# Four buffers for raw expert weights, the root ahead of the low halves, indices copied early, and the routing of a pair of tiles over two steps

## What is computed

```python
for i in range(DEPTH):                      # DEPTH = 1
    mod = silu(c) @ ada_w[i] + ada_b[i]
    sh1, sc1, g1, sh2, sc2, g2 = split(mod, 6)
    hn = modulate(rmsnorm(x, norm1_g[i]), sh1, sc1)
    y = rglru_mixer(hn, ...)                # ends in (...) @ w_out
    x = x + g1 * y
    hn = modulate(rmsnorm(x, norm2_g[i]), sh2, sc2)
    x = x + g2 * grouped_moe(hn, router_w, router_b, w_gate[i], w_up[i], w_down[i])
return rmsnorm(x, final_norm_g)

def grouped_moe(h, ...):
    probs = softmax(h @ router_w + router_b)
    # best of 4 groups by the sum of its two largest, then the two best experts in it
    gates = ...                             # the two probabilities, normed to sum 1
    act = silu(h @ w_gate) * (h @ w_up) * gates     # for each expert
    return act @ w_down
```

## Time and profile before

| | us |
|---|---|
| three timed runs, median | 1388.31 |
| lowest and highest | 1386.82 and 1388.92 |
| profiled execution | 1389.41 |
| its span, first to last instruction | 1387.8 |
| PE busy in it | 1093.6 (79%) |
| DVE busy | 848.6 (61%) |
| POOL busy | 708.6 (51%) |
| ACT busy | 582.2 (42%) |
| mean granted clock of TensorE | 0.923 |

### The profile page before, as it was taken

The page is one execution under the profiler, slowest core; times in us unless marked ns, Lnnn a source line. Parts: engine busy times, 40 slices in busy tenths (PEclk is TensorE's granted clock), DMA queues, the critical chain, the costliest instruction groups (busy, mean ns, idle before and its releaser), DMA issues. The chain is left out here.

```text
span 1387.8 us, 21239 instructions
## 1 busy us (share of the span) xinstructions
PE 1093.6 (79%) x4860; PEld 878.0 (63%) x4861; DVE 848.6 (61%) x1217; ACT 582.2 (42%) x812; POOL 708.6 (51%) x752
## 2 busy tenths in 40 slices
PE   1359999999999992899999408487668778888881
PEld 0247778778778772788888406366556666666661
DVE  6994666766866845367776763355465655565653
ACT  1455667657667654122222103233343443343421
POOL 0555633633633600226676842156666666666653
PEclk9999999999999996999999658799898999999995
DMA  8446334335334125514545374366567667667642
GB/s 301 154 91 205 97 105 154 118 103 165 110 107 154 46 91 197 214 62 173 199 176 198 151 242 124 101 221 226 193 216 242 211 215 231 226 205 232 218 141 91
DMA packets 146301, 232.62 MB, mean 168 GB/s; under 512 B 34240, under 2 KB 101824, under 8 KB 145616
## 3 DMA queue, kind: packets, MB, share of 16 engines
q1 hardware_dynamic: 111248, 128.20, 28.5%
q0 software_dynamic: 23632, 62.49, 12.5%
q10 hardware_dynamic: 11376, 41.42, 9.2%
HBM read 177.45 MB, written 91.31 MB: 194 GB/s over the span
## 5 line engine op out<-in xcount | busy, mean ns | idle before, releaser
L1594 PE MATMUL e_gu<-w_hi,e_xh 128*128 x312 | 134.4, 431 | 37.0 <-DVE e_xl L1494 21.7
L1412 ACT ACTIVATE w_hi<-w_raw 128x1536 f32 x60 | 88.4, 1486 | 160.2 <-DMA w_raw<-in_moe_w_down_dram 96.8
L1275 POOL TENSOR_TENSOR w_lo<-w_raw,w_hi 128x1536 f32 x30 | 106.7, 3556 | 76.0 <-ACT w_hi L1412 39.0
L1596 PE MATMUL e_gu<-w_hi,e_xl 128*128 x312 | 127.7, 409 | 0.0
L1595 PE MATMUL e_gu<-w_lo,e_xh 128*128 x312 | 127.6, 409 | 0.0
L1157 PE MATMUL po<-wo_hi,b_yh 128*128 128x512 f32 x256 | 104.6, 408 | 27.8 <-DVE wo_lo L983 27.8
L1523 DVE SCALAR_TENSOR_TENSOR e_ob<-e_ab,e_rstd,e_fg 128x1024 f32<-128x1024 f32 x39 | 50.1, 1284 | 115.9 <-POOL e_rstd L1324 113.1
L543 DVE SCALAR_TENSOR_TENSOR XB<-xu,conv_w,XB 128x512 f32<-128x512 f32 x96 | 92.1, 960 | 42.3 <-ACT XB L413 38.7
L1617 PE MATMUL e_pd<-w_hi,e_ah 128*128 x156 | 71.3, 457 | 52.2 <-DVE e_al L1499 33.7
L636 PE MATMUL px<-hT_hi,wx_hi 128*128 128x512 f32 x256 | 101.7, 397 | 5.1 <-DVE wx_lo L477 5.1
L636 PE MATMUL pg<-hT_hi,wg_hi 128*128 128x512 f32 x256 | 104.3, 408 | 0.0
(11 more groups left out here) (272 smaller groups left out, 2862.4 us busy)
## 6 DMA issues: line engine op xcount, KB each, us to landing
e_xg<-hn_slots ACTq DMA_DIRECT2D x40, 512.0 KB, 4.9
e_xa<-x_slots ACTq DMA_DIRECT2D x39, 512.0 KB, 3.9
stg<-in_ada_w_dram POOLq DMA_DIRECT2D x32, 512.0 KB, 4.2
w_raw<-in_moe_w_gate_dram SPq DMA_DIRECT2D x32, 384.0 KB, 4.3
w_raw<-in_moe_w_up_dram SPq DMA_DIRECT2D x32, 384.0 KB, 5.0
n_ada<-in_ada_w_dram SPq DMA_DIRECT2D x16, 512.0 KB, 5.1
n_x<-in_x_dram SPq DMA_DIRECT2D x16, 512.0 KB, 3.3
hn_slots<-in_x_dram SPq DMA_DIRECT2D x16, 512.0 KB, 5.0
```

What stands on the lines that cost most here:

```text
L1275: tensor_tensor(w["lo"][:, ds(off + q * QW, QW)], w["raw"][:, q % 2], w["hi"][:, ds(off + q * QW, QW)].bitcast(F32), ALU.subtract).then_in ...
L1412: nc.scalar.activation(w["hi"][:, ds(off + q * QW, QW)], w["raw"][:, q % 2], ACT.Copy).then_inc(w["hi_done"], 1)
L1594: nc.tensor.matmul(gu[:], xh[:, tok], hi, start=(k == 0), stop=False)
L1596: last = nc.tensor.matmul(gu[:], xl[:, tok], hi, start=False, stop=(k == KD - 1))
```

## The change

- There are four raw weight buffers, one for each quarter. SyncE's loads of quarters 2 and 3 of expert 1 wait for nothing, and later quarters wait for the low half of the same quarter of the expert before. In the router stage the two added buffers lie over the projection's weights, so that quarters 2 and 3 of expert 0 are loaded behind the last `main`.
- In the expert stage GpSimd's root has four steps (the small constant of the norm is a column of its own behind e_ab, summed with the squares) and stands ahead of GpSimd's low half. The index columns are copied by `take_indices`, behind the low half, for the block to come.
- In the router stage DVE makes the logits of tile `s-1` in step `s`, behind `scale`; `softmax_in` and `choose` follow in even steps, `assign` and TensorE's `rank` come in odd steps. GpSimd sends one tile in each step, one step earlier than before. Behind the loop DVE makes the low halves of quarters 0 and 1 ahead of the last logits, and the last shift itself; quarters 2 and 3 are both DVE's, behind the tables. The residual rows of the last two tiles are sent last.

```diff
-            for s in range(1, NT + 1):
-                ...
+            for s in range(1, NT):
                 gate(s - 1)
-                if s >= 2:
-                    logits(s - 2)
-                if s >= 3 and s % 2 == 1:
-                    softmax_in((s - 3) // 2)
                 if s + 1 < NT:
                     low(s + 1)
                 if s >= 3 and s % 2 == 1:
-                    choose((s - 3) // 2)
-                if s >= 4 and s % 2 == 0:
-                    assign((s - 4) // 2)
-                if s < NT:
-                    scale(s - 1)
+                    assign((s - 3) // 2)
+                scale(s - 1)
+                logits(s - 1)
+                if s % 2 == 0:
+                    softmax_in(s // 2 - 1)
+                    choose(s // 2 - 1)
             g = NT // 2 - 1
+            gate(NT - 1)
+            low_w(0)
+            low_w(1)
             logits(NT - 1)
             softmax_in(g)
+            choose(g)
             scale(NT - 1)
-            choose(g)
+            dve.wait_ge(scaled, NT)
+            v.tensor_tensor(hn[:, (NT - 1) % RING], hn[:, (NT - 1) % RING], sh2[:], ALU.add).then_inc(last_shifted, 1)
             assign(g)
...
             for s in range(1, NT):
                 root(s - 1)
-                if s >= 5 and s % 2 == 1:
-                    send(s - 5)
-                if s >= 6 and s % 2 == 0:
-                    send(s - 5)
+                if s >= 4:
+                    send(s - 4)
                 shift(s - 1)
...
-                if s >= 4 and s % 2 == 0:
-                    rank((s - 4) // 2)
+                if s >= 3 and s % 2 == 1:
+                    rank((s - 3) // 2)
                 turn(s - 1)
...
             for q in range(2, NQ):
-                sp.wait_ge(w["lo_done"][q % 2], 3)
                 load_quarter(sp, io, w, 1, q)
             for b in range(E, MAXB):
                 load_rec(b)
             for e in range(2, E):
                 for q in range(NQ):
-                    sp.wait_ge(w["lo_done"][q % 2], 2 * e + q // 2)
+                    sp.wait_ge(w["lo_done"][q % 2], 2 * e - 1 + q // 2)
                     load_quarter(sp, io, w, e, q)
...
+                nc.gpsimd.tensor_tensor(root0[:], ssq[:], nhalf[:], ALU.pow).then_inc(rstd_step, 1)
...
+                nc.gpsimd.tensor_scalar(part[:], root0[:], ssq[:], root0[:], ALU.mult, ALU.mult).then_inc(rstd_step, 1)
...
+                nc.gpsimd.tensor_scalar(part[:], part[:], -0.5, 1.5, ALU.mult, ALU.add).then_inc(rstd_step, 1)
...
+                nc.gpsimd.tensor_tensor(rstd[:], root0[:], part[:], ALU.mult).then_inc(rstd_ready, 1)
...
-            with pool.Fori(3, nless) as i:
-                scatter_out(i - 2)
-                scatter_acc(i - 1)
-                low_w(pool, nc.gpsimd.tensor_tensor, i + 1, 1)
-                root(i - 1)
+            with pool.Fori(2, nless) as i:
+                scatter_out(i - 1)
+                scatter_acc(i)
+                root(i)
+                low_w(pool, nc.gpsimd.tensor_tensor, i + 2, 1)
+                take_indices(i + 1, i)
```

More of the change, by code:

```diff
@@ L861, in _ @@
                 squares(s - 1)
-                if s >= 3 and s % 2 == 1:
-                    exponent((s - 3) // 2)
                 evacuate(s - 1)
+                if s < NT and s % 2 == 0:
+                    exponent(s // 2 - 1)
             act.wait_ge(mm, NT)
             high_w(0)
+            high_w(1)
             exponent(NT // 2 - 1)
-            for q in range(1, NQ):
+            for q in range(2, NQ):
                 high_w(q)
@@ L1059, in _ @@
             done(v.tensor_scalar(tab["expert1"][:], eb[:], 1.0, None, ALU.add))
[L1060 to L1064, removed]
+            low_w(2)
+            low_w(3)
         @block.gpsimd
@@ L1113, in _, with send @@
             rows = lambda t: bass.IndirectOffsetOnAxis(ap=t, axis=0)
-            def send(it):
+            def send(it, rest=True):
                 r = it % RING
@@ L1125, in _ @@
                 root(s - 1)
-                if s == 5:
+                if s == 4:
                     pool.wait_ge(filled, 16)
-                if s >= 5 and s % 2 == 1:
-                    send(s - 5)
-                if s >= 6 and s % 2 == 0:
-                    send(s - 5)
+                if s >= 4:
+                    send(s - 4)
                 shift(s - 1)
-                if s == NT - 1:
-                    send(s - 4)
+            send(NT - 4)
             root(NT - 1)
-            send(NT - 4)
-            shift(NT - 1)
-            for it in range(NT - 3, NT):
-                send(it)
-            q = 2
-            pool.wait_ge(w["hi_done"], q + 1)
-            wcols = slice(q * QW, (q + 1) * QW)
-            nc.gpsimd.tensor_tensor(w["lo"][:, wcols], w["raw"][:, q % 2], w["hi"][:, wcols].bitcast(F32),
-                                    ALU.subtract).then_inc(w["lo_done"][q % 2], 1)
+            send(NT - 3)
+            for it in (NT - 2, NT - 1):
+                send(it, False)
+            for it in (NT - 2, NT - 1):
+                send_x2(it)
             for r in range(RING):
@@ L1200, in _ @@
                 main(s, 1, range(KD // 2, KD)).then_inc(mm, 1)
-            rank(NT // 2 - 2)
             turn(NT - 1)
@@ L1274, in low_w @@
                     eng.nop(nofuse=True)
-                    tensor_tensor(w["lo"][:, ds(off + q * QW, QW)], w["raw"][:, q % 2],
+                    tensor_tensor(w["lo"][:, ds(off + q * QW, QW)], w["raw"][q][:],
                                   w["hi"][:, ds(off + q * QW, QW)].bitcast(F32),
@@ L1419, in square @@
                 act.nop(nofuse=True)
-                nc.scalar.activation(squares[:], ab[:], ACT.Square, scale=1.0 / 32, accum_out=ssq[:]).then_inc(squared, 1)
+                if first:
+                    act.wait_ge(halved, 2)
+                nc.scalar.activation(squares[:], ab_eps[:], ACT.Square, scale=1.0 / 32, accum_out=ssq[:]).then_inc(squared, 1)
             load_h(0)
@@ L1683, in build @@
             w["y" + n[0]] = [over(f"b_y{n[0]}{u}", [P, D], (KD + u) * D) for u in range(2)]
+            if n == "lo":
+                w["raw"] += [over(f"w_raw{q}_0", [P, QW], WE + (q - 2) * QW, F32) for q in (2, 3)]
             for i, name in enumerate(("gy", "hT") if n == "hi" else ("g1row", "sh2")):
```

116 lines of the change are left out of this document (62 added, 54 removed).

## The result

The changed kernel takes 1420.38 us (median of four, 1417.57 to 1423.09), the kernel before 1388.62 beside it (1386.82 to 1390.25): a ratio of 1.0229, 95% interval 1.0202 to 1.0256. The forecast was 1401 with a range up to 1416. The direction was right, the time is 19 us beyond the forecast and outside the range. The profiled execution took 1418.5 us with a span of 1417.0, 29.2 more than the span before.

A forecast was written before the change was run, and what follows sets the result against it. TensorE was taken to bound the router stage, GpSimd's queue and its lock with DVE the expert stage. From 1389.4, terms 31.9 + 6 - 4.6 - 9.7 + 5 - 15 - 1 gave 1402.0, forecast 1401 us, range 1352 to 1416.

The forecast's parts named there:

- In the walk: Expert stage: engine chains followed through the new order, giving +5 for two-block experts, -15 for three-block ones, -1 at the drain.
- Router loop: Router stage: choose spills past the next gate and is stopped by GpSimd's shift, 31.9 us, plus 6 for the clock.
- The signs that it named: Profile afterwards: TensorE waits at turn and rank, choose instructions over 2 us, router stage some 38 us longer.
- I take 1 us for each of the six long waits: Router loop: the turn runs slower at the lower granted clock after long waits, 6 us, between 0 and 10.
- End of the router stage: DVE's chain behind the last matmul gets shorter: -4.6 us, between -8 and 0.
- Start of the expert stage: With four buffers SyncE's records and loads wait for nothing and end sooner behind the barrier: -9.7 us.
- ScalarE's waits for weights are worth nothing in a step: Expert stage: removing ScalarE's 96.8 us of weight waits alone gains nothing, since GpSimd's own queue starts its next low half.
- pairs (+5): Expert stage, about nine experts of two blocks: no gain expected, +5 us, from -5 to +12.
- 33.5 us for three steps instead of 36.4: Expert stage, some five experts with a third block, where GpSimd without a low half catches up: -15 us.
- the lock costs more than it did: Rival, expert stage: every e_ob is caught, paired steps take 14.5 us, three-block experts gain nothing; 1425 us, chance 0.09.
- The rival of 1349: Expert steps escape the DVE-GpSimd lock and cost GpSimd's own work alone, 4.9 us less a pair; chance 0.16.

The follow-up runs named there:

- early copies alone: The kernel before with only the index columns copied behind the root for the block to come, ahead of both scatters: 1360.62 us, ratio 0.9804.
- two buffers: The kernel before, two raw buffers kept, with GpSimd's root in four steps behind its low half and index copies a block ahead: 1349.29 us, ratio 0.9718.
- root behind: The changed kernel with its router loop put back and GpSimd's root put back behind its low half: 1335.46 us, ratio 0.9624.
- old loop: The changed kernel with its router loop put back as in the kernel before, all else kept: 1379.37 us, ratio 0.9934.
- e1: The changed kernel with only its router loop put back; router tail, four buffers and expert stage stay: 1379.37 us, ratio 0.9934.
- the second experiment: The changed kernel with GpSimd's shift moved ahead of its sends in the router loop: 1393.72 us, ratio 1.0053.
- the first experiment: The changed kernel with the router loop of the kernel before, its tail, buffers and expert stage unchanged: 1379.37 us, ratio 0.9934.

## Why the prediction was right in direction and too small in size

The runs split the change, along one path. Each line is the difference of two ratios, times 1387 us, and by their intervals uncertain by some 5 us. "In the walk" means that the prediction has no price of its own for the part: it walked through all of the expert stage's steps at once and came to -11 us.

| part of the change | from, to | us | forecast |
|---|---|---|---|
| index copies a block ahead | before, early copies alone | -27 | in the walk |
| root in four steps | early copies alone, two buffers | -12 | in the walk |
| four buffers, new end of the router stage | two buffers, root behind | -13 | -14.3 |
| root ahead of the low half | root behind, old loop | +43 | in the walk |
| router loop | old loop, changed kernel | +41 | +37.9 |
| sum | | +32 | +12.6 |

The three parts in the walk come to +4 us for -11. By the two traces the sum is 16.6 us above the forecast's (29.2 for 12.6): 1.4 us from before the router loop, 2.3 from the loop, 1.8 from the end of the router stage, 1.5 from the wait for records, and 9.6 from the rest of the expert stage.

**Router loop: right in mechanism and in sum, with two errors that cancel.** The signs that it named are there: waits at rank and turn in six steps, a small instruction of `choose` of 3 us, a loop 40 us longer. Its makeup was different. The stall is 3.9 us and not 4.9, since `choose` alone spills 1.3 to 1.7 us and not 2.5; six of them and a first of 1.3 make 25 us for 31.9. The clock took nearly all of the rest, some 14 us for the 6 reckoned: besides the turn the half main behind it ran slowly, 3.7 to 4.6 us instead of 3.0, so that each long wait cost some 2.4 us more. The term "I take 1 us for each of the six long waits" was mis-sized, and its upper end of 10 too. That the loop came out 2 us from its 37.9 is luck: 7 too many for the stall, 8 too few for the clock.

**End of the router stage: right in sign.** -2.8 us for -4.6 (the prediction's own items against it, 2 + 1.3 + 1.3 - 2.9, make 1.7 and not 2.0). Low halves and tables were done at 856.2, but the barrier let go at 863.9; before it GpSimd's ten scatters of the last pair were issued up to 853.1. That their landing ends the stage now is read from this order, no run tested it.

**Start of the expert stage: right.** DVE's wait fell from 19.85 to 11.03, TensorE's start moved 8.2 us for 9.7. 16 records in 17.52 us and 32 in 36.24 are 1.1 us each, and nothing else is left of it.

**ScalarE's waits for weights are worth nothing in a step: right.** 85.7 us of them are in a kernel that is 2.8% faster than before. The one place where two buffers still cost is the expert with a single block, 3.1 us.

**Expert stage: the step that failed.** The prediction walked through the new order as a whole and found nothing for pairs (+5) and, for an expert with a third block, "33.5 us for three steps instead of 36.4", -15 in all. Pairs came out right: 27.3 to 28.6 us between scatters of the output, 27.3 to 28.2 before. The three-block experts take 34.4 to 38.4 us, all seven together 258.9 where they took 257.6: nothing is gained. (There are seven of these and six pairs, where the prediction said five and nine.) With the part of the stage before and behind them, the term of -11 us measured -1.4. What the walk lacked is the far end of e_ob: its buffer is released by a scatter that is now issued behind the low half, and DVE waits 27.9 us for such landings in the whole run, where it waited for none before. It also took e_ab at 1.23 us, where it is 2.39 in the mean. The run with e_y in PSUM shows what that costs: with e_ab free, the seven take 244.8 us instead of the 259.4 of e1. What the late scatter costs apart from e_ob's own stop stays open. The rival *the lock costs more than it did* gave 1425, 5 us from the result, but partly by chance: it charged 19 us to pairs, which cost nothing more, left out half of the clock, and took 10 us for the lost gain of the three-block experts, where the forecast's own term was 15. What it had right is that the three-block experts gain nothing.

**What the walk hid.** The worse mistake is not in the result but in the reasoning: moving the root and moving the copies were costed as one, "it is inside these walks". Apart, they are +43 and -27 us. By the prediction's own rows a step of GpSimd lost 0.2 + 0.87 us by the copy ahead of the sum's scatter; times 26 steps with weights that is 28 us, and the early copies alone measured 27.

**The rival of 1349** (steps free of the lock) wanted GpSimd's low half less than 8 us behind e_ob. The order with the root behind meets that (5.8 us, 1104.59 to 1110.43), as the kernel before did (7.7 us). In the changed kernel it starts 11.2 us behind the e_ob of 1172.22, for 9.8 reckoned, so late that it runs into the next e_ob and e_ab (1183.41, 0.8 us behind that e_ob's start). With the early copies and four buffers the order of before gives 1335 us: the move of the root took away the condition on which this rival stood.

## What to carry to other kernels

An instruction that locks another engine out is placed by what the other engine does at that moment: GpSimd's low half is free beside DVE's work with an operand in PSUM and costs 3 us beside work on two SBUF operands. 43 us hung on the order of one queue, by the lock and by the late scatter together. Cost each moved step alone before you walk through all of them together; two edits of opposite sign hide each other. A wait of an engine that disappears (here DVE's for the root) is worth nothing if that engine does not set the step, and a scatter that is issued late holds its source buffer: e_ob waited 3.61 us for one.

## What was not expected of the hardware

- With one operand in PSUM DVE's addition of 128x1024 takes 1224 ns in the mean, where it took 1.23 us unstopped: leaving the lock costs nothing of its own.
- In the changed kernel's loop the granted clock fell after all six waits of TensorE of 2.5 us; in the second experiment it fell after two of seven waits of 1.3 to 1.7 us, with nothing in the rows that tells the two from the five. The fall lasts into the matmuls behind the turn, and costs about as much again as the wait at the turn. It doesn't always come at once: behind the loop of the first experiment the turn that followed a wait of 2.78 us ran in 1.09 us at a granted clock of 1.00, and only the matmuls from 779 us on were at 0.50.
- GpSimd's root of one element a partition took 2.22 us beside DVE's two low halves, for 0.57 to 0.62 where DVE has no such work, and DVE's instruction of 8 elements 2.95 us for 0.17. The Trainium skill ("SBUF — State Buffer", Who interferes with whom) says that of two such instructions the later one is blocked until the first has finished, and that one with a single SBUF input is not concerned. By the second rule, the traces agree (e_ab, 1224 ns). By the first, they agree for e_ab, which starts 0.74 us behind GpSimd's low half (1184.15 and 1183.41); but the small DVE instructions, here and in rows 4, are blocked although their records start 0.5 to 0.7 us ahead of GpSimd's (725.06 and 725.57), so for them the order in the trace does not tell which one is blocked.
